# Group phases of a hybrid decoder step: another order of eight units, and two smaller edits

## Chip, cores and metric

One NeuronCore of one Trainium2 chip runs the whole kernel. The metric is device time in microseconds (us), the median of three runs.

## What is computed

One layer of a hybrid decoder for a prompt (256 tokens) and 8 sequences of 8 tokens (64 samples), 320 columns in all, in float32. The change touches the Mamba-2 (SSD) branch alone. Cut to that:

```python
xbc, _ = causal_conv(xbc, sconv0, s_conv_w, s_conv_b)      # 24 tiles of 128 channels, 4 taps
xbc = silu(xbc)
xs, Bm, Cm = xbc[..., :2048], xbc[..., 2048:2560], xbc[..., 2560:]     # 4 groups of 8 heads of 64
cum = cumsum(dt * A)                                        # per head
lmat = exp(where(mask, cum[:, None] - cum[None, :], -inf))
cb = einsum('btgn,bsgn->btsg', Cm, Bm)
y = einsum('btsg,btsge,bsgep->btgep', cb, lmat, xs * dt) + exp(cum) * (Cm @ h)
h_new = exp(cum[-1]) * h + einsum('bsgn,bsge,bsgep->bgepn', Bm, exp(cum[-1] - cum), xs * dt)
gated = (y + D * xs) * silu(z)                              # then a norm per group, and w_pb
merged = sigmoid(ga) * ya + sigmoid(gb) * yb                # then w_out
```

x, z, xbc, ga and gb all come from products with slices of one weight matrix `w_in`.

## The kernel before

Activations lie with channels on 128 partitions and the 320 columns along the free dimension. A *unit* is one 128-channel output tile of a product with weights: `dense` (24 matmuls of 128x320: high weights by high input, high by low, low by high, since each float32 factor is split in two rounded parts). The list of units, in the order in which they run, is written by hand in `unit_order`; every engine loops over the same list. PE's queue is in order: a unit's matmuls, then what was placed behind that unit. In the loops over units, ScalarE (ACT) makes the high half of the weights two units ahead once the current unit is done (`high_ahead`, line 1541), then empties the unit's PSUM bank; VectorE (DVE) makes the low half behind it (`low_ahead`, line 2113). Each panel of weights (two units) is brought by SyncE's queue (SP) into one of four ring slots once the slot's last unit has its low half.

Four *group phases*, one for each SSD group `gr`, run from 724 to 941 us, eight units each (`PHASE_UNITS`, `four_each`). Phase 0: four units of xbc, then ga 0 to 3; phases 1 and 2: four of xbc, then z 0 to 3 or 4 to 7; phase 3: gb 0 to 3, then z 8 to 11. The four xbc units are convolved for the next group. An xbc unit costs ACT two copies into a padded buffer (`conv`), POOL three small copies (`conv_side`, lines 669 to 678), DVE four operations of 128x344 (`conv`, lines 2281 to 2285), and ACT a Silu in two pieces (`conv_silu`, lines 1684 and 1685), issued four units later. A gate unit (ga, z) costs ACT one activation into one of two buffers `gate_tmp` (`gate`, line 1896) and DVE one product (`gated`, line 2553). gb units are kept unopened.

Behind the units of a phase PE has the group's own work, by position `i` of the unit:

- `i` = 0: `group_rows`: inputs turned, the products cb, B turned; DVE makes xd (line 2615), xd_s (2621), and masked cb (`masked_scores`, 2646 to 2649).
- `i` = 0 to 3: `decay_rows(i)` for two heads; ACT takes three exponentials a head (`head_weights`, 1944 to 1946); DVE multiplies them by cb (`weights`, 2658 and 2660).
- `i` = 1 to 4: `head_outputs(i - 1)`, which waits for `weights(i - 1)`; DVE reads it out in `outputs` (2666).
- `i` = 1, DVE: `old_part` of the group before, `sample_masks` (2630 to 2637); `i` = 2, PE: `grown_decays`.
- `i` = 4 to 7: `sample_states(i - 4)`, of which the first waits for `outputs(3)`, the others for `update` of the step before (DVE, eight operations, 2681); POOL sends each updated state (line 787); `i` = 5: `prompt_states`.

SP loads the states of the next group into the four buffers that POOL has sent, in front of the panels named in `states_before`.

In `head_outputs` the two heads of a pair write the two halves of the partitions. The prompt's parts have 128 rows; the samples' part has 64: `xd_s[0:64]` by `w[0:64, 384:448]`. Each float32 matmul shows as two in the profile.

Of the kernel before, what the change touches and what calls it, by code (L numbers as in the profile page):

```python
# [6 lines left out]
ACT = mybir.ActivationFunctionType  # L7
# [128 lines left out]

def unit_order():
# [13 lines left out]
    order += [u for phase in PHASE_UNITS for u in four_each(phase)] + four_each(TAIL_UNITS)  # L151
# [30 lines left out]
def build(nc, io, out):  # L182
# [5 lines left out]
    with ctx:  # L188
# [292 lines left out]
        def phase_units(gr):  # L481
            return [st.at[name, q] for name, q in four_each(PHASE_UNITS[gr])]
# [23 lines left out]
        def _(sp_):  # L506
# [49 lines left out]
            states_before = {("xbc", 2): (0, 1, 2, 3), ("z", 2): (4, 5), ("xbc", 12): (6,), ("xbc", 14): (7,), ("z", 6): (8, 9),  # L556
# [33 lines left out]
        def _(pool):  # L590
# [184 lines left out]

            picks(0, 0)
            for gr in range(SG):
                for i, u in enumerate(phase_units(gr)):
                    if u.name == "xbc":
                        conv_side(u, pad2, 3)  # L780
                    if i < 4 and (gr, i) != (SG - 1, 3):
                        picks(gr + (i + 1) // 4, (i + 1) % 4)
                for j in range(4):
                    n = 4 * gr + j
                    pool.wait_ge(S["up_done"], n + 1)
                    for s in range(2):
                        pool.dma_start(h_of(out["s_ssm"], j + 4 * s, gr), four(state_of(n, s))).then_inc(state_out[n % 4], 16)
                    if j == 1:
                        pool.wait_ge(S["ph_copied"], gr + 1)
                        pool.dma_start(h_of(out["p_ssm"], 0, gr), four(prompt_h)).then_inc(prompt_sent, 16)  # L790
# [29 lines left out]
        def _(pe):  # L820
# [506 lines left out]
            def head_outputs(gr, i):  # L1327
# [15 lines left out]
                for o, col, w in heads:  # L1343
                    ins = mm(b[o, 256:320], xd_s[0:64, col], w[0:64, 384:448], False, True)
# [178 lines left out]
        def _(act):  # L1523
# [373 lines left out]

            def kept_gate(u, func):
                act.wait_ge(unit_done, u.done)
                nc.scalar.activation(merged_g[:, u.own, :], bank_of(u), func).then_inc(bank_free[u.bank], 1)  # L1900
# [32 lines left out]
            def head_weights(gr, i):  # L1933
# [6 lines left out]
                for e in range(2):  # L1940
# [5 lines left out]
                    nc.scalar.activation(w[0:64, 384:448], aux[e][0:64, 384:448], ACT.Exp, bias=g3[0:64, 2, 4 + h:5 + h]).then_inc(S["w_exp"], 1)  # L1946
# [17 lines left out]
            for gr in range(SG):  # L1964
                us = phase_units(gr)
                for i, u in enumerate(us):
# [9 lines left out]
                    else:  # L1976
                        gate(u, ACT.Sigmoid if u.name == "ga" else ACT.Silu)
# [16 lines left out]
                    if i >= 4:  # L1994
                        if us[i - 4].name == "xbc":
                            conv_silu(us[i - 4], acc2, xbc_t)
# [93 lines left out]
        def _(dve):  # L2090
# [488 lines left out]
            def decay_halves():  # L2579

                ch.inc(V.tensor_copy(cum_rows[64:96, 0:256], aux[0][0:SH, 0:256]))
# [69 lines left out]
            def weights(gr, i):  # L2651

                dve.wait_ge(S["w_exp"], 8 * gr + 2 * i + 2)
                if i == 0:
# [3 lines left out]
                ch.inc(V.scalar_tensor_tensor(out=w[:, :, 0:384], in0=w[:, :, 0:384], scalar=1.0, in1=c[:, :, 0:384].to_broadcast([128, 2, 384]),  # L2658
                                              op0=ALU.min, op1=ALU.mult))
                V.scalar_tensor_tensor(out=w[0:64, :, 384:448], in0=w[0:64, :, 384:448], scalar=1.0, in1=c[0:64, :, 384:448].to_broadcast([64, 2, 64]),  # L2660
                                       op0=ALU.min, op1=ALU.mult).then_inc(S["w_ready"], 1)
# [35 lines left out]
            for gr in range(SG):  # L2697
                for i, u in enumerate(phase_units(gr)):
                    low_ahead(u)
                    if u.name == "xbc":  # L2700
                        conv(u, pad2, 3, acc2, 216, 240, 24)
# [11 lines left out]
                    if i == 4:  # L2713
                        weighted_inputs(gr)
                    if i >= 4:
                        update(gr, i - 4)
                        gated(u, ya if u.name == "ga" else xbc_t)
# [38 lines left out]
            dve.wait_ge(S["gate_open"], 1)  # L2756
# [75 lines left out]
```

## Time and profile before

| | us |
|---|---|
| median of 3 runs (lowest, highest) | 1340.95 (1337.51, 1342.23) |
| the profiled execution's own time | 1340.6 |
| its span | 1338.9 |
| TensorE (PE) busy | 1272.0, 95% |
| VectorE (DVE) busy | 768.1, 57% |
| ScalarE (ACT) busy | 617.7, 46% |
| GpSimd (POOL) busy | 215.4, 16% |

The span is the time between the first and the last instruction. The 1.7 us between span and time lie outside. A row of a timeline gives the start and length of a run of equal instructions, and in brackets how long the engine sat idle before it and whose result released it. `arena` is one large buffer that holds most of the branch's tiles, so its name says little; the line tells the operation.

### The profile page before, as it was taken

How to read it: one execution, taken by the hardware profiler on the slowest of the kernel's cores; microseconds unless marked ns; L12 is line 12 of the kernel's file. 1: busy time of each engine (PE TensorE's matmuls, PEld its weight loads, DVE VectorE, ACT ScalarE, POOL GpSimd, SP SyncE). 2: the span in 40 equal slices, each digit the busy share in tenths (PEclk: the TensorE clock that was granted, in tenths of full speed). 3: DMA queues.
4: the chain of work that ended last, by engine and by line, in shares of the span. 5: the costliest groups of instructions: out<-in, count | busy, mean ns of one | idle time of the engine just before them, and what ended most of it. 6: DMA issues, size and time to landing. Idle time of an engine off the chain costs nothing. (4 is left out here: it accounts for less than half of the span.)

```text
span 1338.9 us, 22662 instructions
## 1 busy us (share of the span) xinstructions
PE 1272.0 (95%) x9096; PEld 1157.1 (86%) x9096; DVE 768.1 (57%) x1340; ACT 617.7 (46%) x1066; POOL 215.4 (16%) x377
## 2 busy tenths in 40 slices
PE   6899999998999999989999999999999999999997
PEld 3799999997997776668998888888989979999997
DVE  1644445336885565655379786865665565545433
ACT  3433333334667554644355664554652343333443
POOL 3100000001540321211024242321500010000010
PEclk9899999998999999999999999999999989999999
DMA  9957677785443688893764355473436465544551
GB/s 301 265 182 230 221 221 212 224 235 179 127 127 127 199 273 291 290 282 106 203 196 128 119 173 167 134 213 114 126 94 189 142 205 158 154 137 131 152 149 42
DMA packets 258862, 241.56 MB, mean 180 GB/s; under 512 B 8607, under 2 KB 242479, under 8 KB 258710
## 3 DMA queue, kind: packets, MB, share of 16 engines
q1 hardware_dynamic: 249262, 211.03, 52.0%
q0 software_dynamic: 9024, 28.91, 6.3%
q8 instruction: 73, 1.20, 0.4%
q10 hardware_dynamic: 472, 0.17, 0.1%
q14 instruction: 31, 0.25, 0.1%
HBM read 209.88 MB, written 30.21 MB: 179 GB/s over the span
## 5 line engine op out<-in xcount | busy, mean ns | idle before, releaser
L2113 DVE TENSOR_TENSOR w_lo<-ring,w_hi 128x1024 fp32r<-128x1024 f32 (+1 forms) x264 | 336.8, 1277 | 421.1 <-ACT w_hi L1541 420.6
L1541 ACT ACTIVATE w_hi<-ring 128x1024 fp32r<-128x1024 f32 (+1 forms) x264 | 289.3, 1097 | 532.3 <-PE bank L826 526.2
L826 PE MATMUL bank<-u_hi,w_hi 128*128 128x320 f32 x1536 | 275.4, 323 | 9.6 <-ACT u_hi L1566 5.1
L826 PEld LDWEIGHTS bank<-u_hi,w_hi 128*128 128x128 f32 x1536 | 238.2, 193 | 28.3 <-issue 19.5
L826 PE MATMUL bank<-u_lo,w_hi 128*128 128x320 f32 x1536 | 257.6, 310 | 0.0
L826 PE MATMUL bank<-u_hi,w_lo 128*128 128x320 f32 x1536 | 257.0, 310 | 0.1
L826 PEld LDWEIGHTS bank<-u_lo,w_hi 128*128 128x128 f32 x1536 | 234.8, 189 | 0.0
L826 PEld LDWEIGHTS bank<-u_hi,w_lo 128*128 128x128 f32 x1536 | 233.7, 188 | 0.6 <-DVE w_lo L2113 0.4
L628 POOL TENSOR_TENSOR arena<-arena 128x320 f32<-128x320 f32 x24 | 21.0, 874 | 611.8 <-ACT arena L1553 598.8
L823 PE MATMUL aux<-ident,arena 128*128 128x128 f32 (+6 forms) x404 | 61.8, 278 | 17.3 <-ACT arena L1598 8.7
L826 PE MATMUL bank<-arena 32*128 32x128 f32 (+5 forms) x536 | 57.5, 376 | 15.1 <-DMA arena<-in_state_mlstm_C 7.9
L823 PEld LDWEIGHTS aux<-ident,arena 128*128 128x128 f32 (+6 forms) x404 | 44.8, 143 | 30.5 <-issue 16.0
L826 PE MATMUL bank<-ff_hi,w_hi 128*128 128x320 f32 x352 | 58.5, 314 | 0.0
L826 PE MATMUL bank<-ff_lo,w_hi 128*128 128x320 f32 x352 | 56.8, 309 | 0.0
L826 PE MATMUL bank<-ff_hi,w_lo 128*128 128x320 f32 x352 | 56.8, 309 | 0.0
L826 PEld LDWEIGHTS bank<-arena 32*128 32x128 f32 (+3 forms) x536 | 30.4, 155 | 30.5 <-issue 17.8
L826 PEld LDWEIGHTS bank<-ff_hi,w_hi 128*128 128x128 f32 x352 | 52.3, 188 | 2.5 <-issue 2.5
L826 PEld LDWEIGHTS bank<-ff_lo,w_hi 128*128 128x128 f32 x352 | 52.9, 188 | 0.0
L826 PEld LDWEIGHTS bank<-ff_hi,w_lo 128*128 128x128 f32 x352 | 52.9, 188 | 0.0
L2283 DVE SCALAR_TENSOR_TENSOR arena<-arena,par 128x344 f32<-128x344 f32 x80 | 46.6, 583 | 6.6 <-POOL arena L675 4.3
L1527 ACT ACTIVATE arena<-bank 128x256 f32<-128x256 f32 (+4 forms) x138 | 44.4, 352 | 12.8 <-PE bank L826 9.4
L826 PE MATMUL bank<-y_hi,w_hi 128*128 128x320 f32 x256 | 43.2, 310 | 2.3 <-ACT w_hi L1541 1.3
(363 smaller groups left out, 1513.0 us busy)
## 6 DMA issues: line engine op xcount, KB each, us to landing
ring<-in_w_in SPq DMA_DIRECT2D x52, 1024.0 KB, 5.4
ring<-in_ff_w SPq DMA_DIRECT2D x44, 1024.0 KB, 5.5
ring<-in_ada_w SPq DMA_DIRECT2D x36, 1024.0 KB, 7.4
ring<-in_ff_w SPq DMA_DIRECT2D x32, 704.0 KB, 4.9
arena<-in_state_mlstm_C SPq DMA_DIRECT2D x32, 512.0 KB, 5.6
out_s_C<-arena POOLq DMA_DIRECT2D x32, 512.0 KB, 5.7
ring<-in_w_pa SPq DMA_DIRECT2D x8, 1024.0 KB, 8.1
arena<-in_state_ssm SPq DMA_DIRECT2D x32, 256.0 KB, 4.3
```

The source lines that it names most:

```text
L628: ins = nc.gpsimd.tensor_tensor(sq[:, 0, :], sq[:, 0, :], sq[:, kc, :], ALU.add)
L823: return nc.tensor.transpose(dst, src, ident[0:rows, 0:rows])
L826: return nc.tensor.matmul(dst, lhs, rhs, start=first, stop=last)
L1527: return nc.scalar.activation(dst, src, ACT.Copy, scale=scale)
L1541: nc.scalar.activation(w_hi[v.split_no % 2][:, 0:v.kc, :], panel_part(v), ACT.Copy).then_inc(S["hi_done"], 1)
L2113: V.tensor_tensor(w_lo[r][:, 0:v.kc, :], panel_part(v), w_hi[r][:, 0:v.kc, :].bitcast(FP32), ALU.subtract)\
L2283: ch.link(V.scalar_tensor_tensor(out=a, in0=p[:, tap:tap + CONVW], scalar=par[:, c + w_col + tap * tiles:c + w_col + tap * tiles + 1], in1 ...
```

## The change

Three edits.

1. Order. In phases 0 to 2 the two first gate units come first, then the four xbc units, then the other two gate units. Phase 3 stays. The first two gates are copied out of PSUM unopened; ACT opens them in place (Sigmoid or Silu) at `i` = 4, and DVE applies them at `i` = 5. At `i` = 4 DVE convolves behind `outputs(3)` and `weighted_inputs`, at `i` = 5 in front of `update(1)`. The Silus of the convolved tiles come at `i` = 5, 6 and (two) 7. POOL sends the first state at `i` = 5 in front of that unit's share of the convolution. The state loads keep their places in SP's queue.
2. The weights of a pair of heads are multiplied in one operation of 128x896 in place of one of 128x768 and one of 64x128.
3. For that, the samples' part of `head_outputs` has 128 rows, the exponentials of the samples run over 128 rows, and the lower halves of `xd_s` and of the samples' part of cb are cleared once (`decay_halves`).

```diff
+def phase_order(phase):
+    own, other = phase[0], phase[1]
+    if own[0] != "xbc":
+        return four_each(phase)
+    rest = four_each((other,))
+    return rest[0:2] + four_each((own,)) + rest[2:4]
...
-            states_before = {..., ("z", 2): (4, 5), ("xbc", 12): (6,), ("xbc", 14): (7,), ...
+            states_before = {..., ("z", 2): (4, 5), ("z", 4): (6,), ("xbc", 12): (7,), ...
...
 POOL, in the phases
+                    if i == 5:
+                        send_state(gr, 0)
                     if u.name == "xbc":
                         conv_side(u, pad2, 3)
...
-                for j in range(4):
+                for j in range(1, 4):
+                    send_state(gr, j)
...
 PE, head_outputs
-                    ins = mm(b[o, 256:320], xd_s[0:64, col], w[0:64, 384:448], False, True)
+                    ins = mm(b[o, 256:320], xd_s[:, col], w[:, 384:448], False, True)
...
 ACT
-                    nc.scalar.activation(w[0:64, 384:448], aux[e][0:64, 384:448], ACT.Exp, bias=g3[0:64, 2, 4 + h:5 + h]).then_inc(S["w_exp"], 1)
+                    nc.scalar.activation(w[:, 384:448], aux[e][:, 384:448], ACT.Exp, bias=g3[:, 2, 4 + h:5 + h]).then_inc(S["w_exp"], 1)
...
-                        gate(u, ACT.Sigmoid if u.name == "ga" else ACT.Silu)
+                        gate(u, ACT.Copy if i < 4 else gate_func(u))
...
-                    if i >= 4:
-                        if us[i - 4].name == "xbc":
-                            conv_silu(us[i - 4], acc2, xbc_t)
+                    if i == 4 and gr < SG - 1:
+                        for v in us[0:2]:
+                            x = gate_tmp[:, gate_no[v.n] % 2, :]
+                            nc.scalar.activation(x, x, gate_func(v)).then_inc(S["gate_open"], 1)
+                    if gr < SG - 1 and i >= 5:
+                        for v in us[i - 3:i - 2] if i < 7 else us[4:6]:
+                            conv_silu(v, acc2, xbc_t)
...
 DVE, decay_halves
+                ch.inc(V.memset(xd_s[64:128, :], 0.0))
+                ch.inc(V.memset(cbm[64:128, 384:448], 0.0))
...
 DVE, weights
-                ch.inc(V.scalar_tensor_tensor(out=w[:, :, 0:384], in0=w[:, :, 0:384], scalar=1.0, in1=c[:, :, 0:384].to_broadcast([128, 2, 384]), ...))
-                V.scalar_tensor_tensor(out=w[0:64, :, 384:448], in0=w[0:64, :, 384:448], scalar=1.0, in1=c[0:64, :, 384:448].to_broadcast([64, 2, 64]), ...)
+                V.scalar_tensor_tensor(out=w, in0=w, scalar=1.0, in1=c.to_broadcast([128, 2, 448]), op0=ALU.min, op1=ALU.mult).then_inc(S["w_ready"], 1)
...
 DVE, in the phases
-                    if u.name == "xbc":
+                    if u.name == "xbc" and i != 4:
                         conv(u, pad2, 3, acc2, 216, 240, 24)
...
                     if i == 4:
                         weighted_inputs(gr)
+                        if u.name == "xbc":
+                            conv(u, pad2, 3, acc2, 216, 240, 24)
                     if i >= 4:
                         update(gr, i - 4)
+                    if i == 5 and gr < SG - 1:
+                        for n, v in enumerate(phase_units(gr)[0:2]):
+                            dve.wait_ge(S["gate_open"], 2 * gr + n + 1)
+                            gated(v, ya if v.name == "ga" else xbc_t)
+                    if i >= 4 and u.name != "xbc":
                         gated(u, ya if u.name == "ga" else xbc_t)
```

## Rows read from the trace of the kernel before

**Rows 1.** The page, part 1: busy time and share of the span by engine.

```profile
...
PE 1272.0 (95%) x9096; PEld 1157.1 (86%) x9096; DVE 768.1 (57%) x1340; ACT 617.7 (46%) x1066; POOL 215.4 (16%) x377
...
```

**Rows 2.** Stretches of the span: phase 1.

```profile
...
777.80:833.00 55.20, 52.14 (x451) 45.90 (x450) 40.67 (x86) 28.41 (x67) 18.45 (x30) 1.00 0.52 158
...
```

**Rows 3.** Waits of PE from 723 to 942 us: total, times, longest (us).

```profile
...
PE bank L826 <- DVE arena L2660: 5.5, 8, 1.1
...
PE aux L826 <- DVE w_lo_rest L2637: 0.7, 2, 0.3
```

**Rows 4.** PE timeline: start, length, engine, line, operation, tiles [idle before <-releaser].

```profile
...
723.89 1.09 PE L823 MATMUL aux<-ident,arena 128*128 128x128 f32 x8 [1.78 <-ACT arena L1685]
...
732.72 0.87 PE L826 MATMUL bank<-arena 128*64 128x256 f32 x8 [0.88 <-DVE arena L2660]
...
777.85 1.04 PE L823 MATMUL aux<-ident,arena 128*128 128x128 f32 x8
...
787.02 0.87 PE L826 MATMUL bank<-arena 128*64 128x256 f32 x8 [1.06 <-DVE arena L2660]
...
793.69 0.87 PE L826 MATMUL bank<-arena 128*64 128x256 f32 x8 [0.38 <-DVE arena L2660]
...
804.29 0.87 PE L826 MATMUL bank<-arena 128*64 128x256 f32 x8 [0.57 <-DVE arena L2660]
...
806.74 0.49 PE L826 MATMUL bank<-arena 32*128 32x128 f32 x4 [0.29 <-DVE arena L2666]
```

**Rows 5.** DVE timeline in phase 1, iterations 0 and 1.

```profile
...
780.35 0.47 DVE L2281 TENSOR_SCALAR arena<-arena,par 128x344 f32<-128x344 f32 x1
...
782.58 1.28 DVE L2615 TENSOR_TENSOR arena<-aux,sp 128x512 f32<-128x512 f32 x2
...
785.82 0.96 DVE L2658 SCALAR_TENSOR_TENSOR arena<-arena 128x768 f32<-128x768 f32 x1
786.69 0.28 DVE L2660 SCALAR_TENSOR_TENSOR arena<-arena 64x128 f32<-64x128 f32 x1
...
```

**Rows 6.** ACT timeline: end of phase 0 and iteration 0 of phase 1.

```profile
...
775.83 1.28 ACT L1684 ACT_TABLE_LOAD   x1
...
777.45 0.24 ACT L1685 ACTIVATE arena<-arena 128x64 f32<-128x64 f32 x1
...
784.03 0.31 ACT L1946 ACTIVATE arena<-aux,g 64x64 f32<-64x64 f32 x1
...
```

**Rows 7.** PE timeline, one head output and the unit behind it.

```profile
743.98 0.60 PE L826 MATMUL bank<-arena 128*64 128x256 f32 x6
744.51 0.33 PE L826 MATMUL bank<-arena,xd_s 64*64 64x64 f32 x4
744.77 0.41 PE L826 MATMUL bank<-u_hi,w_hi 128*128 128x320 f32 x1
```

**Rows 8.** Groups of DVE by line and shape, the whole span: a clearing.

```profile
...
L2559 DVE MEMSET sp<- 64x32 f32 x1 | 0.1, 85 | 0.1
...
```

**Rows 9.** DVE timeline in the first eight convolved units: low halves.

```profile
...
685.99 1.22 DVE L2113 TENSOR_TENSOR w_lo<-ring,w_hi 128x1024 fp32r<-128x1024 f32 x1
...
709.44 1.22 DVE L2113 TENSOR_TENSOR w_lo<-ring,w_hi 128x1024 fp32r<-128x1024 f32 x1
...
719.79 1.23 DVE L2113 TENSOR_TENSOR w_lo<-ring,w_hi 128x1024 fp32r<-128x1024 f32 x1
...
```

**Rows 10.** DVE timeline in phase 0: the updates of iterations 4 and 5.

```profile
...
752.77 2.15 DVE L2681 SCALAR_TENSOR_TENSOR arena<-arena,h_dec,bank 128x128 f32<-128x128 f32 x8 [0.21 <-PE bank L826]
...
760.97 2.16 DVE L2681 SCALAR_TENSOR_TENSOR arena<-arena,h_dec,bank 128x128 f32<-128x128 f32 x8 [0.51 <-PE bank L826]
...
```

**Rows 11.** POOL timeline in phase 0: sending the first states.

```profile
...
755.50 1.60 POOL L787 DMA_DIRECT2D out_s_ssm<-arena  x2 [8.55 <-DVE arena L2681]
...
```

**Rows 12.** PE timeline in phase 0: second and third sample states.

```profile
...
759.76 1.16 PE L826 MATMUL bank<-arena 32*128 32x128 f32 x16
...
766.16 1.16 PE L826 MATMUL bank<-arena 32*128 32x128 f32 x16
...
```

More of the change, by code:

```diff
@@ L150, in unit_order @@
     order += [("xbc", q) for q in XBC_FIRST]
-    order += [u for phase in PHASE_UNITS for u in four_each(phase)] + four_each(TAIL_UNITS)
+    order += [u for phase in PHASE_UNITS for u in phase_order(phase)] + four_each(TAIL_UNITS)
     order += [("pb", q) for q in PART_ORDER]
@@ L481, in phase_units @@
         def phase_units(gr):
-            return [st.at[name, q] for name, q in four_each(PHASE_UNITS[gr])]
+            return [st.at[name, q] for name, q in phase_order(PHASE_UNITS[gr])]
         def tail_units():
@@ L554, in state_loads @@
                     sp_.dma_start(four(state_of(n, s)), h_of(io["state_ssm"], j + 4 * s, gr)).then_inc(state_in[r], 16)
-            states_before = {("xbc", 2): (0, 1, 2, 3), ("z", 2): (4, 5), ("xbc", 12): (6,), ("xbc", 14): (7,), ("z", 6): (8, 9),
+            states_before = {("xbc", 2): (0, 1, 2, 3), ("z", 2): (4, 5), ("z", 4): (6,), ("xbc", 12): (7,), ("z", 6): (8, 9),
                              ("gb", 0): (10,), ("gb", 2): (11,), ("z", 10): (12, 13), ("z", 12): (14,), ("z", 14): (15,)}
@@ L774, in picks, with send_state @@
                 pool.wait_ge(S["masks_ready"], MH + n + 1)
+            def send_state(gr, j):
+                n = 4 * gr + j
+                pool.wait_ge(S["up_done"], n + 1)
+                for s in range(2):
+                    pool.dma_start(h_of(out["s_ssm"], j + 4 * s, gr), four(state_of(n, s))).then_inc(state_out[n % 4], 16)
             picks(0, 0)
@@ L782, in _ @@
                         picks(gr + (i + 1) // 4, (i + 1) % 4)
-                for j in range(4):
[L784 to L787, printed above, removed]
+                for j in range(1, 4):
+                    send_state(gr, j)
                     if j == 1:
@@ L1896, in gate, with gate_func @@
                 nc.scalar.activation(gate_tmp[:, i % 2, :], bank_of(u), func).then_inc(bank_free[u.bank], 1)
+            def gate_func(u):
+                return ACT.Sigmoid if u.name == "ga" else ACT.Silu
             def kept_gate(u, func):
@@ L2657, in weights @@
                 c = cbm.unsqueeze(1)
[L2658 to L2661, printed above, removed]
+                V.scalar_tensor_tensor(out=w, in0=w, scalar=1.0, in1=c.to_broadcast([128, 2, 448]), op0=ALU.min, op1=ALU.mult).then_inc(S["w_ready"], 1)
             def outputs(gr, i):
@@ L2755, in _ @@
                 group_norm_low(c)
-            dve.wait_ge(S["gate_open"], 1)
+            dve.wait_ge(S["gate_open"], 2 * SG - 1)
             def merge(u):
```

## The prediction, made before the changed kernel ran

> **What bounds the kernel now.** I read the page first. PE is busy 95% of the span and no other engine above 57% [rows 1], so the order of PE's own queue sets the end, and time is won only where PE waits or where its own work gets shorter. Then I took the stretches of the four group phases. The reader is to see 55.2 us for phase 1 with 52.1 us of PE in it at a granted clock of 1.00, with DVE the next busiest [rows 2]: some 3 us a phase are not PE's, and the clock has nothing to give back there. Then PE's waits in the phases, where two groups matter: 5.5 us in 8 waits for the weights' second operation (line 2660) and 0.7 us in 2 for line 2637, the rows of `grown_decays` [rows 3]. Then PE's timeline, to place them [rows 4]: phase 0 has one of 0.88 us at the first head output; phase 1 has 1.06 (head output 0), 0.38 (head output 1), 0.57 (head output 3) and 0.29 (first sample states), and phase 2 repeats phase 1 to a hundredth. Phase 0 has the 0.57 and the 0.29 too. The last reading is why `weights` is late: in phase 1's iteration 0 DVE convolves from 780.35 to 782.58 (2.23 us), and only then reads the group's rows, with the weights' first operation at 785.82 and the second ending at 786.97 [rows 5], while the exponentials had ended at 784.34 [rows 6]. The convolution stands in front of the work that PE waits for.
>
> **The order of the units, what it removes.** In iterations 0 and 1 of phases 0 to 2 DVE loses one convolution each, 2.23 us. A gate unit there costs DVE nothing, and ACT one copy in place of two.
> Phase 1, iteration 0: weights(0) would start at 785.82 - 2.23 = 783.6, but the exponentials end at 784.34, so it starts near 784.4 and ends near 785.5. PE was ready for head output 0 at 787.02 - 1.06 = 785.96 [rows 4 to 6]. The wait of 1.06 goes, with 0.5 us to spare; next in line are the exponentials, in time.
> Iteration 1: DVE again is 2.23 us earlier. weights(1), whose end let PE start at 793.69, comes near 791.4. PE, without its waits of 1.06, 0.35 (0.7 in 2, [rows 3]) and 0.38, gets there near 793.69 - 1.79 = 791.9; the rows of `grown_decays` stand a weights operation ahead of it, and PE asks for them 0.7 us ahead, so they are as much in time. Both waits go, again by about 0.5 us.
> Phase 0: the 0.88 goes in the same way. Sum: 0.88 + 2 x (1.06 + 0.38) + 0.7 = 4.46 us, say 4.5.
>
> **What of the waits stays.** Iteration 3 still holds a convolution: ACT's high half, DVE's low half, 2.23 us of convolution and the weights follow the end of unit 3 as before, so head output 3 still waits about 0.57 us in phases 0 to 2. Behind it the first sample states wait for outputs(3), and that stands behind the low half that begins when unit 4 is done. So what head output 3 gains by itself is lost 1 us later in the 0.29 [rows 4]. I count nothing for either.
>
> **Where the convolutions go.** Iteration 4: 2.23 us now lie in front of update(0). It ran from 752.77 to 754.92 in phase 0 [rows 10]; it will end near 757.1, and PE wants it at 759.76, behind unit 5 and the prompt's states [rows 12]. Cover 2.6 us. Iteration 5: conv in front of update(1), which was done at 763.1 after 0.51 us of waiting [rows 10] and will be at 764.9 to 765.4; PE wants it at 766.16 [rows 12]. Cover 0.8 to 1.3 us. If either cover went, the excess would be paid once in each of three phases. The two late products of the opened gates (0.5 us each) come behind update(1), ahead of a low half that can't start before ACT has seen the unit in front of 766.16 done: nothing.
> POOL: sending the first states takes 1.60 us from 755.50 [rows 11]; it will start near 757.1 and stands in front of unit 5's history copy (an estimated half microsecond, by the length of such short POOL work), which ends near 759.2. DVE wants it behind its low half, at 760.97 - 0.51 = 760.46 [rows 10]. Cover 1.2 us. SP: the loads stand at the same panels, and their buffers are sent at most 2 us later; they are used a phase later. Nothing.
> ACT: the opening of two gates at iteration 4 is one table load (1.28, [rows 6]) and two activations of half a microsecond, 2.3 us; a Sigmoid's table load, gate and tile's Silu stood there before, and DVE asks for the gates only a unit later. Nothing. At iteration 7 there are two tiles of Silu where there was one. In phase 0 the gate there is a Sigmoid, so a table load from 775.83 stands ahead of the Silu, whose last piece ends at 777.69; PE turns the rows at 777.85 without a wait [rows 4, 6]. The tile took 777.69 - 775.83 - 1.29 = 0.57 us, and one more behind it, overlapping by 0.1, brings the end to 778.15 to 778.2: PE waits about 0.35 us. In phases 1 and 2 gate and Silu share a table and the 1.28 us are not there, so 0.9 us of room is left. Cost 0.35 us, once.
> A rule of the Trainium skill speaks against this place (page "ScalarE: Activation LUTs", section "What ACT_TABLE_LOAD costs"): a switch costs 1.28 us and then a drain of 1.38 us. By that, iteration 7 with its two switches could not be over by 777.69 as it is. The trace has 1.28 us of load and the function right behind it, so I take the row; with the page's price PE's wait there would be 3.1 us and the whole gain about 2.1 us.
>
> **The one operation of weights.** 128x896 in one is about 0.07 us shorter than the two, by the distance from 785.82 to the end at 786.97 (1.15 us) against the first operation's rate (some 1.09). It ends in waits that are gone or re-anchored: nothing on the path. Bounds: 0 to 16 x 0.07 = 1.1 us; I take 0.
>
> **The 128 rows of head outputs.** PE runs the samples' part as 64*64 tiles between 128*64 tiles and 128*128 ones. In the row group of six, the last pair starts at 744.58 - 0.27 = 744.31, and pairs of 128 columns follow each other by 0.11, as in the run of eight of 1.04 us ((1.04 - 0.27) / 7 = 0.11). The next would start at 744.42; the 64*64 pair starts at 744.51 [rows 4, 7]. So 0.09 us goes with the change of tile shape. With 128 rows the shape is that of the pair before, and only the change to 128*128 behind it is left. That counts in front of a unit or a re-anchored wait, so for head outputs 0, 1 and 2 of each phase, not 3: 12 x 0.09 = 1.1 us. The trace of before has no 128*64 pass behind another one on 64 columns in this place, so bounds: gain up to 0.20 us each (the whole distance), 2.4 us; loss of 0.02 each (longer weight loads), 0.2 us. I take 1.1, the measured gap.
> The Trainium skill has this as a rule (page "TensorEngine Tiling (Array Packing)", section "Key Properties"): changing the tiling mode, not just the tile, drains TensorE. The trace agrees with a gap of 0.09 us at each change; by the rule alone the gain would have the same sign and no size.
>
> **The clearing.** Two new DVE operations of 512 and 64 columns in front of the first convolution. The nearest row clears 64x32 in 0.085 us [rows 8]; at about 1 ns a column that is 0.5 to 0.7 us in all. DVE there runs back to back: from 685.99 to 709.44 it needs 3.35 us a unit, against PE's 3.52, and it only just catches up: from 709.44 to 719.79 are 10.35 us where three periods are 10.05 [rows 9]. That is 0.3 us of slack before the last convolution, whose Silu PE waits for at 723.89. So 0.3 to 0.4 us comes through; I take 0.35. Bounds 0 and 0.7.
>
> **The sum.** -4.5 - 1.1 + 0.35 + 0.35 = -4.9 us. Made against the profiled execution's own 1340.6 us (span 1338.9 and 1.7 around it) that is 1335.7; the median of the three runs is 0.35 higher, so 1336.0. Behind the phases nothing is anchored to an outside clock: weights are loaded when slots come free, and the shift is carried to the end.
>
> **Rivals.**
> A. *The tile change gives nothing* (the gap belongs to the short 64-column pass and not to the shape). For: the gap is seen only ahead of 64 columns in this place. Against: all changes of shape have a gap like it. Sum -3.8: 1337.1.
> B. *The stalls move to head output 2 and 3.* With iterations 0 and 1 free of waits, PE reaches the units with convolutions sooner. From the end of unit 2, ACT's high half is about 1.2 us, DVE's low half and convolution 3.35 [rows 9], the weights 1.09: 5.7. PE needs 787.02 to 793.69 less its 0.73 of waits, 5.9, and two more decay products, 6.4. Were DVE 1.5 us later than that, 0.8 us would return in each of three phases: -2.5, 1338.4. Against: both are counted from the same unit's end, and their lengths repeat from phase to phase.
> C. *The gain is absorbed behind the phases*, in a wait for weights or states: about 1340. For: SP's queue holds loads behind states that POOL must have sent. Against: with 3 us of PE's waits a phase [rows 2], the weights were there each time.
> D. *Slower.* POOL now sends states in front of a history copy that DVE's convolution of unit 5 needs, and update(1) is behind that. Place: iteration 5 of phases 0 to 2. Free until the send is 1.2 us later than I have it, and PE feels it 0.9 us later still. From 2.1 us PE waits one for one, three times; to lose more than 4.9 us, each send has to be 3.7 us late, so to take 5.3 us for 1.6. For: POOL's operations vary with DVE at work. Against: the sends are 1.5 to 1.6 throughout. Price then 1342 and more.
>
> **Chances.** Forecast 0.60, A 0.14, B 0.12, C 0.08, D 0.06. I predict 1336.0. The forecast's own range is 1334.5 to 1337.5; with A, B and part of C, and the bounds of tile change and clearing, 1333.8 to 1339.8. 0.3% is 4.0 us and about what a measurement of this kernel can tell from no change: faster by more needs under 1336.9. Most of the forecast and a little of A lie there: 0.56; the same 0.38; slower 0.06.
>
> **What would show it.** Right: PE has no wait at head outputs 0 and 1 in phases 0 to 2; it keeps 0.5 to 0.6 at head output 3 and 0.2 to 0.4 at the first sample states; a new wait of some 0.35 us on line 1685 at phase 1's rows; the first one, 1.78 us, grows to 2.1; the samples' part starts 0.11 behind the pair before it; phases 1 and 2 take 53.1 us for 55.2. Wrong: waits on the weights at head output 2, waits of `sample_states` for an update, DVE waiting for POOL at unit 5, or phases shorter by less than 1.5 us.

## The result and the profile after

| | before | after |
|---|---|---|
| median (lowest, highest; runs), us | 1339.57 (1335.23, 1342.23; 8) | 1331.95 (1325.47, 1339.78; 8) |
| the profiled execution's own time | 1340.6 | 1333.15 |
| its span | 1338.9 | 1331.4 |
| mean granted clock of TensorE | 0.985 | 0.986 |

The ratio is 0.9947 (95% interval 0.9929 to 0.9966): 7.6 us faster, between 4.6 and 9.5. The forecast of 1336.0 us had the direction right; the time is 1.85 us below its range. The kernel before has a median of 1339.57 now that it has 8 runs, 1.4 us less than the 1340.95 of the three that I worked from.

The page of the changed kernel answers to [rows 1]: PE is 3.0 us less busy, the span is 7.5 us shorter.

```profile
...
PE 1269.0 (95%) x9096; PEld 1156.7 (87%) x9096; DVE 767.7 (58%) x1326; ACT 618.0 (46%) x1070; POOL 205.8 (15%) x377
...
```

The stretches of the changed kernel, as in [rows 2]: phases 0 to 3 and then the twelve units up to `w_pb` (the tail). Columns: stretch and length, then PE, PEld, DVE, ACT and POOL busy (instructions), granted clock, DMA share, GB/s. Each phase begins where the next pass of PE could start behind the last unit before it.

```profile
...
720.09:776.52 56.43, 52.85 (x449) 46.76 (x447) 41.18 (x83) 36.28 (x75) 14.91 (x29) 0.97 0.40 124
776.52:829.65 53.13, 51.52 (x451) 46.02 (x450) 40.43 (x82) 29.63 (x71) 15.02 (x30) 1.00 0.56 162
829.65:882.37 52.72, 51.29 (x451) 45.96 (x449) 40.43 (x82) 29.37 (x69) 15.01 (x30) 1.00 0.56 170
882.37:935.32 52.95, 51.44 (x453) 46.16 (x451) 32.34 (x66) 26.48 (x55) 8.69 (x16) 1.00 0.52 155
935.32:987.48 52.16, 48.91 (x338) 47.17 (x336) 31.81 (x49) 34.85 (x54) 18.10 (x22) 1.00 0.43 125
...
```

Before, the same stretches were 55.90, 55.16, 55.15, 53.41 and 53.18 us, at clocks of 1.00, 1.00, 1.00, 1.00 and 0.97. Phase 0 and the tail of the kernel before:

```profile
...
721.95:777.85 55.90, 51.96 (x449) 45.65 (x448) 41.18 (x87) 38.18 (x76) 15.70 (x29) 1.00 0.42 128
...
941.57:994.75 53.18, 50.43 (x339) 48.69 (x337) 32.98 (x51) 35.75 (x55) 18.11 (x22) 0.97 0.43 126
...
```

Phases 1 and 2 are 2.0 and 2.4 us shorter; phase 1 takes the 53.1 us forecast for both, phase 2 0.4 us less. Phase 0 is 0.5 us *longer*, at a clock of 0.97, though its wait of 0.88 us at the first head output is gone. And the tail, in which the change moves nothing, is 1.0 us shorter, with its clock at 1.00 now.

PE's waits from 715 to 940 us, with the columns of [rows 3]. Of the 5.5 us in 8 waits on `weights`, 2.0 us in 3 are left (line 2681 is the one operation now), and the 0.7 us on the rows of `grown_decays` are gone.

```profile
...
PE aux L837 <- ACT arena L1699: 2.3, 2, 2.1
PE bank L840 <- DVE arena L2686: 2.2, 4, 1.1
PE bank L840 <- DVE arena L2681: 2.0, 3, 0.7
...
```

PE's timeline, as in [rows 4, 7]: the rows of phase 0 and what follows them, head output 3 and the first sample states of phase 0, the rows of phase 1, and a head output of phase 3.

```profile
...
722.39 1.14 PE L837 MATMUL aux<-ident,arena 128*128 128x128 f32 x8 [2.14 <-ACT arena L1699]
723.33 1.06 PE L837 MATMUL bank<-ident,arena 128*64 128x128 f32 x4
724.18 1.89 PE L840 MATMUL bank<-arena 128*128 128x256 f32 x6
...
747.89 0.87 PE L840 MATMUL bank<-arena 128*64 128x256 f32 x8 [0.66 <-DVE arena L2681]
...
750.25 1.16 PE L840 MATMUL bank<-arena 32*128 32x128 f32 x16 [0.35 <-DVE arena L2686]
...
776.87 1.09 PE L837 MATMUL aux<-ident,arena 128*128 128x128 f32 x8 [0.18 <-ACT arena L1699]
...
890.41 0.87 PE L840 MATMUL bank<-arena 128*64 128x256 f32 x8
891.11 0.28 PE L840 MATMUL bank<-arena,xd_s 128*64 128x64 f32 x4
891.33 0.85 PE L840 MATMUL bank<-u_hi,w_hi 128*128 128x320 f32 x4
```

The same six products at phase 0's rows in the kernel before, behind its wait of 1.78 us:

```profile
...
725.26 1.08 PE L826 MATMUL bank<-arena 128*128 128x256 f32 x6
...
```

The reader is to see four things. The first wait is 2.14 us for the 1.78 of [rows 4], as forecast. No wait is left at head outputs 0 to 2; the two forecast to stay are there. The samples' part of head outputs (64 columns) has the shape of the pairs in front of it and starts 0.70 us after the first of them. And the six products at 724.18 take 1.89 us, for 1.08 before (725.26). That last row is what the forecast had no term for. The stretch from 723.3 to 726.7 of the changed kernel, with the columns of the stretches above, is at half clock (1.2 GHz for 2.4):

```profile
...
719.00:723.30 4.30, 2.16 (x17) 1.89 (x16) 2.64 (x5) 1.52 (x4) 2.15 (x5) 1.00 0.62 191
723.30:726.70 3.40, 3.40 (x16) 2.73 (x14) 3.38 (x5) 0.31 (x1) 0.00 (x0) 0.50 0.21 67
726.70:730.00 3.30, 2.87 (x18) 2.57 (x18) 0.89 (x4) 3.05 (x8) 0.58 (x2) 1.00 0.01 2
```

PE had sat idle for 2.14 us before it. In the kernel before, the wait there was 1.78 us and the clock stayed at full; its only fall between 720 and 1050 us is at 990.9, in the tail, behind waits of 1.01, 0.25 and 1.49 us.

Beside PE, in the changed kernel: DVE's weights(0) of phase 0 and its convolution at iteration 5, POOL's send and the history copy that rival D named, and ACT's Silus at the end of phase 0.

```profile
...
730.56 1.09 DVE L2681 SCALAR_TENSOR_TENSOR arena<-arena 128x896 f32<-128x896 f32 x1 [2.97 <-ACT arena L1963]
...
759.04 0.47 DVE L2302 TENSOR_SCALAR arena<-arena,par 128x344 f32<-128x344 f32 x1
...
756.08 1.60 POOL L789 DMA_DIRECT2D out_s_ssm<-arena  x2 [6.25 <-DVE arena L2701]
757.67 0.22 POOL L677 COPY arena<-hist 128x24 f32<-128x24 f32 x1
...
774.50 1.28 ACT L1698 ACT_TABLE_LOAD   x1
775.79 0.42 ACT L1698 ACTIVATE arena<-arena 128x256 f32<-128x256 f32 x1
...
776.57 0.24 ACT L1699 ACTIVATE arena<-arena 128x64 f32<-128x64 f32 x1
...
```

And the two clearings, by group (mean in ns):

```profile
...
L2602 DVE MEMSET xd_s<- 64x512 f32 x1 | 0.5, 485 | 0.2 <-issue 0.2
...
L2603 DVE MEMSET arena<- 64x64 f32 x1 | 0.1, 112 | 0.0
...
```

### The profile page after: what moved, and what is told of

Its sections match the earlier page's. It is cut to its first block, busy times and chain, and to the rows that moved or that the text cites. A ratio compares the mean times of both kernels' runs of the same rounds, so it can differ in the third digit from the quotient of the medians.

```text
span 1331.4 us, 22658 instructions
## 1 busy us (share of the span) xinstructions
PE 1269.0 (95%) x9096; PEld 1156.7 (87%) x9096; DVE 767.7 (58%) x1326; ACT 618.0 (46%) x1070; POOL 205.8 (15%) x377
## 4 chain that ended last, share of the span: by engine, by line
PE 55%; DVE 7%; ACT 4%; DMA 3%; issue 2%; POOL 0%; ACTq 0%; DVEq 0%; POOLq 0%
PE bank L840 47%; PE aux L840 6%; DVE w_lo L2134 2%; PE aux L837 2%; DMA arena<-in_state_mlstm_C 2%; ACT w_hi L1555 1%; DMA out_s_C<-arena 1%; DVE arena L2304 1%; DVE arena L2504 1%; PE bank L837 1%; ACT arena L1541 0%; ACT kp L1541 0%; DVE arena L2302 0%; DVE stats L2528 0%; ACT vp L1541 0%
```

## Experiments

Times are medians; the ratio is to the kernel before on the same chip. Since single executions scatter by 5 to 14 us, I read the terms from the profiles: "phases" is the sum of the four, "rest" the length from the start of phase 0 to the end of the last matmul (the kernel ends 6.5 to 6.9 us behind it in every profile). Before: phases 219.62, rest 610.26. After: 215.23 and 604.76.

| run | median (runs) | ratio, interval | phases 0, 1, 2, 3 | tail | rest |
|---|---|---|---|---|---|
| e1_after_again | 1332.39 (6) | 0.9955, 0.9941 to 0.9970 | 56.43 53.13 52.73 52.95 | 51.68 | 604.26 |
| e2_order_only | 1333.71 (6) | 0.9961, 0.9946 to 0.9976 | 54.95 53.58 53.18 53.39 | 53.69 | 606.28 |
| e3_rows_only | 1339.21 (12) | 0.9997, 0.9984 to 1.0011 | 57.14 54.75 54.75 52.94 | 52.31 | 610.13 |
| e4_clear_early | 1332.96 (6) | 0.9948, 0.9930 to 0.9965 | 54.51 53.12 52.74 52.95 | 53.70 | 604.39 |
| e5_fill_rows | 1333.93 (12) | 0.9963, 0.9946 to 0.9981 | 55.74 53.13 52.73 52.95 | 52.13 | 604.03 |
| e6_fill_all | 1330.68 (8) | 0.9941, 0.9919 to 0.9963 | 55.74 in phase 0 | 52.61 | 603.77 |
| e7_conv_late | 1329.67 (6) | 0.9935, 0.9915 to 0.9955 | 54.40 52.26 52.25 52.35 | 51.43 | 599.99 |
| e8_all | 1331.24 (7) | 0.9948, 0.9929 to 0.9968 | 54.74 52.27 52.27 52.36 | 52.61 | 600.85 |
| e9_late_early | 1330.83 (6) | 0.9913, 0.9882 to 0.9944 | 54.03 52.25 52.26 52.35 | 52.19 | 600.37 |
| e10_fill_sized | 1329.80 (6) | 0.9909, 0.9886 to 0.9933 | 54.04 52.25 52.26 52.35 | 51.57 | 599.06 |
| e11_two_weights | 1337.32 (1) | one run | 56.54 53.12 52.73 52.95 | 53.70 | 606.55 |

**e1_after_again**: the changed kernel, no edit, to learn how much of the result repeats.

> The changed kernel once more, for its spread and for the granted clock of each run. Theory (fixed gain in the phases plus TensorE's clock): between runs the time moves with the mean granted clock by about 1.6 us for 0.001, as the eight runs so far do (1325.5 us at 0.991, 1339.8 us at 0.982); the median is 6 to 8 us under before, and at equal clock the distance is 5 to 6 us. In the phases of its trace the only waits are again 0.65 us at head output 3, 0.35 at the first sample states (three times each), 0.2 at phase 1's rows and about 2.1 at phase 0's rows. Rival (all of the 7 us is fixed work saved): the distance at equal clock is 7 to 8 us.

Measured: 6.4 us under the kernel before (4.0 to 7.9). The phases repeat to a hundredth, the fall of the clock behind the first wait with them, and the tail again has no fall. The 17 executions of the kernel before on this chip and the 6 of this run have nearly the same mean clock (0.9866 and 0.9863) and mean times of 1338.6 and 1333.0 us. Within the runs of one kernel the time moves by some 1.4 us for 0.001 of mean clock, so my estimate of the distance at equal clock is 6.0 us, give or take 0.7: the upper end of the 5 to 6 expected.

**e2_order_only**: the changed kernel with the second and third edit taken back.

```diff
-                    ins = mm(b[o, 256:320], xd_s[:, col], w[:, 384:448], False, True)
+                    ins = mm(b[o, 256:320], xd_s[0:64, col], w[0:64, 384:448], False, True)
...
-                ch.inc(V.memset(xd_s[64:128, :], 0.0))
-                ch.inc(V.memset(cbm[64:128, 384:448], 0.0))
...
-                V.scalar_tensor_tensor(out=w, in0=w, ...)
+ (the two operations of before)
```

> Only the order of the units with what goes with it; the two weights operations, the 64-row samples' part and no clearing, as before. Theory: the waits at head outputs 0 and 1 and at grown_decays go (4.5 us), phase 1's rows wait 0.2 us, so 4.3 us under before at equal clock; phases 1 and 2 take 53.3 us where before has 55.2; the wait at phase 0's rows stays 1.78. Rival (the rows edit carries the part that was not forecast): the same 4.3, but then the rows alone give 3.

**e3_rows_only**: the opposite, the kernel before with the second and third edit alone.

> Only the one weights operation, the 128 rows and the clearing, in the old order. Theory: each head output is 0.14 us shorter on PE (0.10 ahead of the samples' part and 0.04 in it), of 16 some 10 to 12 count: 1.4 to 1.7 us, and the wait at phase 0's rows grows by 0.36; the weights end 0.07 us earlier, which shortens seven waits: 0 to 0.5 us. Sum 1.0 to 1.8 us under before at equal clock. Rival: 3 us.

Measured: the order is worth 219.62 - 215.10 = 4.5 us of phases, and 5.1 us of the medians (3.2 to 7.2). The other two edits are worth 0.04 us (219.62 - 219.58), and 0.9997 as a ratio: the 1.0 to 1.8 us expected of them did not come. The stretches show why: first e2_order_only's phases 0, 1 and 3, then e3_rows_only's.

```profile
...
720.17:775.12 54.95, 51.89 (x449) 45.56 (x447) 41.05 (x87) 36.13 (x75) 14.54 (x29) 1.00 0.42 129
775.12:828.70 53.58, 52.11 (x451) 45.94 (x450) 40.66 (x86) 29.48 (x71) 15.02 (x30) 1.00 0.53 160
...
881.88:935.27 53.39, 52.04 (x453) 46.08 (x451) 32.57 (x70) 26.35 (x55) 8.68 (x16) 1.00 0.53 156
...
```

```profile
...
720.38:777.52 57.14, 52.87 (x449) 46.68 (x448) 41.26 (x83) 38.30 (x76) 16.91 (x29) 0.97 0.41 126
777.52:832.27 54.75, 51.50 (x451) 45.95 (x450) 40.45 (x82) 28.53 (x67) 17.85 (x30) 1.00 0.52 159
...
887.02:939.96 52.94, 51.43 (x453) 46.16 (x451) 32.33 (x66) 26.49 (x55) 8.69 (x16) 1.00 0.52 154
...
```

In phase 3, where the order is the old one in both, 128 rows bring 53.41 to 52.94 and 53.39 to 52.95: 0.45 us for three head outputs, 0.15 each. So rival A is out. Phase 0 pays it back: 57.14 for 55.90, with the clock at 0.97, though no order was changed there. So the loss in phase 0 belongs to the third edit.

**e4_clear_early**: the changed kernel; `xd_s` is cleared behind unit 11 of `w_pa`, where DVE waits for about 2 us in each unit.

```diff
-                ch.inc(V.memset(xd_s[64:128, :], 0.0))
...
+                if u.q == 11:
+                    ch.inc(V.memset(xd_s[64:128, :], 0.0))
```

> The changed kernel with the large clearing (64x512) moved from in front of the first convolution to the units of w_pa before. Theory: the wait at phase 0's rows falls back from 2.14 to about 1.8 us; 0.3 us less at equal clock. If the clock falls after waits of PE and a longer wait makes it likelier, the half-clock stretch of 3.4 us that began at 723.3 us in the changed kernel is gone here in the profile and the mean clock of the runs is higher by 0.001 or so. If it is a matter of chance, the stretch may as well stay.

PE's timeline of e4_clear_early at the rows of phase 0:

```profile
...
718.66 1.09 PE L837 MATMUL aux<-ident,arena 128*128 128x128 f32 x8 [1.77 <-ACT arena L1699]
...
720.03 1.08 PE L840 MATMUL bank<-arena 128*128 128x256 f32 x6
...
```

Measured: the wait is back at 1.77, the six products at 1.08, phase 0 at 54.51 for 56.43. Of these 1.92 us, 0.36 is the wait (2.14 - 1.78) and 1.56 the clock. The time of the whole does not follow: the median of 1332.96 us is no lower than the 1332.39 of e1_after_again on the same chip, and the runs' mean clock is 0.9867 for 0.9863, where 0.001 more was expected. In this profile the tail has its fall of the clock again (53.70), as e2_order_only and e11_two_weights have, and before.

**e5_fill_rows**: the changed kernel with the wait left as it is, but with six float32 products in it whose results nothing reads, so that PE isn't idle. It separates "the wait got longer" from "PE idle lets the clock fall".

```diff
+            def fill(bank, n):
+                for k in range(n):
+                    mm(bank[:, 0:T], ones[:, :], x_t[:, 0, :], True, True)
...
                 if gr == 0:
                     pe.wait_ge(S["hd_read"], 1)
+                    fill(aux[2], 6)
+                pe.wait_ge(S["conv_silu"], 28 + 4 * gr)
```

> The changed kernel with six float32 products of 128x320 by ones (12 passes, 1.8 us of PE) put into the 2.1 us in which PE waits at phase 0's rows; their result is overwritten. Theory A (the clock falls because PE sat idle there): the half-clock stretch at 723 us is gone, the phase-0 stretch, 56.43 us from one unit's end to the next, falls to 54.8 to 55.0 although no wait of the data got shorter, and the stretch of half clock in the tail, which before, the order alone and the early clearing had at 980 to 991 us and the changed kernel had not, either comes back (then the two are tied, and nothing is won in all) or stays away (then 1.5 us are won). Theory B (the fall has nothing to do with the idle time): phase 0 stays at 56.4.

PE's timeline of e5_fill_rows:

```profile
...
722.30 3.39 PE L840 MATMUL aux<-x_t,ones 128*128 128x320 f32 x12
725.53 1.04 PE L837 MATMUL aux<-ident,arena 128*128 128x128 f32 x8
726.40 0.60 PE L837 MATMUL bank<-ident,arena 128*64 128x128 f32 x4
726.84 1.08 PE L840 MATMUL bank<-arena 128*128 128x256 f32 x6
...
```

Measured: no fall, with Silu as late as in the changed kernel. But twelve passes take 3.23 us to the next start where the gap was 2.30 (720.09 to 722.39), 0.9 us too long, so phase 0 gains 0.7 and not 1.6. The tail's fall stays away (52.13). So the 1.6 us come with the idle PE and not with the late data: the data are as late here. That rests on this profile and on e6_fill_all, which has the same fill and no fall there either.

**e6_fill_all**: the same fill, and further ones in front of the two norms' first units (8 products each) and of tail units 9 and 11 (4 each), where PE also waits.

> As e5_fill_rows, and the same kind of products in front of the two norms' first units (8 each, where PE waits 2.8 and 2.3 us for the normed input and the clock then falls for 6.8 and 3.4 to 6.8 us) and in front of the tail's units 9 and 11 (4 each, where it waits 1.5 us). Theory A: the half-clock stretches at 317, 723, 985 and 1085 us are gone or shorter, the mean clock goes from 0.987 to 0.993, and the time falls by 5 to 9 us under the changed kernel with no data wait changed. Theory B: the clock falls as before and the time is the same or, where a filler is longer than the wait, up to 1 us more.

Measured: mean clock 0.994 for 0.986 in the profiled executions; the `up2` units went from 158.14 to 156.13 us, but the fills in front of them were longer than the gap (41.12 us from the first unit of `w_out` to the first of `up2`, for 39.54). In all 1.0 us less rest than the changed kernel, and 3.3 us by the medians against e5_fill_rows on the same chip; 5 to 9 had been expected. Much of what the clock gave, the oversized fills took.

**e7_conv_late**: to take the two waits that stay. The convolution of iteration 3 goes behind `outputs(2)`, `outputs(3)` in front of the low half, and the Silus come as 1, 2, 1 at `i` = 5, 6, 7.

```diff
+                    if i == 4:
+                        outputs(gr, 3)
                     low_ahead(u)
-                    if u.name == "xbc" and i != 4:
+                    if u.name == "xbc" and i not in (3, 4):
...
-                    if 1 <= i <= 4:
+                    if 1 <= i <= 3:
                         outputs(gr, i - 1)
+                    if i == 3 and u.name == "xbc":
+                        conv(u, pad2, 3, acc2, 216, 240, 24)
...
-                        for v in us[i - 3:i - 2] if i < 7 else us[4:6]:
+                        for v in us[2:3] if i == 5 else us[3:5] if i == 6 else us[5:6]:
```

> The changed kernel with the two waits that I had let stand taken away: DVE convolves unit 3 behind outputs(2), reads head output 3 out in front of the next low half, and the Silus come one at i = 5, two at 6, one at 7. Theory (these waits are fixed work of DVE in front of what PE waits for): the 0.65 and the 0.35 go in phases 0 to 2, the 1.08 in phase 3, and the 0.18 at phase 1's rows: 4.2 us less; phases 1, 2 and 3 take 52.0, 51.7 and 51.9 for 53.13, 52.73 and 52.95. Rival (update or the convolution of unit 4 is late next): new waits for DVE at the second sample states and less than 2 us.

PE's timeline of e7_conv_late at head output 3 and the first sample states of phase 0:

```profile
...
745.24 0.87 PE L840 MATMUL bank<-arena 128*64 128x256 f32 x8
...
747.86 1.16 PE L840 MATMUL bank<-arena 32*128 32x128 f32 x16 [0.61 <-DVE arena L2686]
...
```

Measured: phases 211.26, 4.0 us under the changed kernel, of which 1.6 is that the clock did not fall behind a wait of 2.15 us in this execution. The other 2.4 us are the edit's own: the wait at head output 3 is gone, phase 1's rows are in time, but 0.61 us now stands at the sample states, since they need `outputs(3)` as soon as PE gets there. A stall moved by one step, and I had not counted it: 4.2 us had been expected, and phases 1, 2 and 3 at 52.0, 51.7 and 51.9 us came out at 52.26, 52.25 and 52.35.

**e8_all**: early clearing, late convolution and the fills (5, 8, 8, 4, 4 products).

> Early clearing, late convolution, spread Silus and the fillers (five in place of six at phase 0's rows) together. If the parts add: 0.35 for the clearing, 4.2 for the waits, 5 to 9 for the clock, 10 to 13 us under the changed kernel and some 18 under before. If the clock falls on its own, 4 to 5 under the changed kernel.

Measured: the parts do not add. The rest is 3.9 us under the changed kernel's (10 to 13 expected), the median 6.6 us under the kernel before (18 expected).

**e9_late_early**: the same without fills.

> The late convolution, the spread Silus and the early clearing together, no fillers. Theory: phase 0 takes 54.0 us (54.41 with the late convolution alone, less 0.35), the others as in e7_conv_late (52.25, 52.25, 52.35); the clock has no fall at phase 0's rows; from the end of the last unit ahead of the phases to the last matmul 599.6 us where the tail keeps full clock and 601.1 where it falls there. The median 1329 to 1331. Rival (the 1.9 us of the clearing in e4 were chance): phase 0 keeps 55.6.

Measured: phase 0 takes 54.03 us, the others what they take in e7_conv_late, and the median is 1330.83, all as expected. The rest is 600.37 for 599.6.

**e10_fill_sized**: with the fills cut to the gaps (3, 4, 4, 2, 2).

> e9 with fillers cut to the waits: a product of 128x320 takes 0.53 us (two passes of 0.27), so 3 at phase 0's rows (1.6 us in 1.9), 4 in front of each of the two norms' first units (2.1 us in 2.8 and 2.3) and 2 in front of each of the two tail units (1.1 us in 1.5). Theory (the idle time lets the clock fall, and the fillers of e6 and e8 gave back 1 us and more each by being longer than the waits): no stretch of half clock at 317, 985 and 1085 us, none of the four waits longer than without fillers, and 3 to 6 us under e9. Rival (a shorter filler leaves enough idle time for the clock to fall): as e9 within 1 us.

Measured: e9's phases are 210.89, 4.3 us under the changed kernel. The fills of e8 cost what they win behind the start of phase 0 (rest 600.85 against 600.37 without). Cut to size they gain there: PE's timeline in front of the first norm's first unit, first e9_late_early, then e10_fill_sized:

```profile
...
320.90 5.48 PE L840 MATMUL bank<-u_hi,w_hi 128*128 128x320 f32 x16 [2.80 <-ACT u_hi L1580]
...
```

```profile
...
317.68 2.32 PE L840 MATMUL aux<-x_t,ones 128*128 128x320 f32 x8
320.65 4.30 PE L840 MATMUL bank<-u_hi,w_hi 128*128 128x320 f32 x16 [0.65 <-ACT u_hi L1591]
...
```

The same 16 passes take 4.30 us for 5.48, and they start as long after the pass before the wait as without the fill. From phase 0 on e10 is 1.3 us shorter than e9; the medians (1329.80 and 1330.83) can't tell them apart, so the 3 to 6 us expected did not come. Ahead of phase 0 this profile has a half-clock stretch at 443.6 us, behind a wait of 1.83 us, that no other profile has. e10_fill_sized has the lowest ratio, with an interval that overlaps those of e7_conv_late and e9_late_early: 10.0 us under the kernel before on its chip, and 5.7 us under the changed kernel by the rest (599.06 for 604.76). Its ratio's interval (0.9886 to 0.9933) just meets that of the changed kernel (0.9929 to 0.9966); the two were not timed on the same chip.

**e11_two_weights**: the changed kernel with the weights' operation cut into 128x768 and 128x128.

```diff
-                V.scalar_tensor_tensor(out=w, in0=w, ...).then_inc(S["w_ready"], 1)
+                ch.inc(V.scalar_tensor_tensor(out=w[:, :, 0:384], in0=w[:, :, 0:384], ...))
+                V.scalar_tensor_tensor(out=w[:, :, 384:448], in0=w[:, :, 384:448], ...).then_inc(S["w_ready"], 1)
```

> The changed kernel with its one weights operation split again in 128x768 and 128x128. Theory (the one operation is off the path): head output 3 waits 0.07 us longer and the first sample states 0.07 less, phases 1 to 3 stay at 53.13, 52.73 and 52.95 us within 0.05. Rival: each of the 16 is paid, 0.07 to 0.3 us a phase more.

PE's timeline of e11_two_weights at head output 3 and the sample states of phase 0:

```profile
...
750.16 0.87 PE L840 MATMUL bank<-arena 128*64 128x256 f32 x8 [0.72 <-DVE arena L2682]
...
752.46 0.79 PE L840 MATMUL bank<-arena 32*128 32x128 f32 x9 [0.28 <-DVE arena L2687]
```

Measured: phases 1 to 3 equal the changed kernel's to a hundredth. Head output 3 waits 0.07 us longer and the sample states 0.07 us shorter (0.72 and 0.28, for 0.66 and 0.35): the one operation is worth nothing on the path. The run's 1337.32 us is one execution, with the tail's fall (53.70) and a half-clock stretch of 6.8 us for 3.4 at the second norm.

## Why the prediction was wrong

**The step that failed** is the last one of the sum, and what it was laid on: "Made against the profiled execution's own 1340.6 us ... that is 1335.7; the median of the three runs is 0.35 higher, so 1336.0", with "the shift is carried to the end" behind it. I gave the unknown costs a width; the base and all that lies outside the phases got none, and the clock got no term at all. The base was 1.4 us high: with 8 runs the kernel before is at 1339.57, and on the other chips at 1338.76, 1337.85 and 1339.80 (17, 20 and 11 runs). That is 1.4 of the miss of 4.05 us. The other 2.7 us are a measured difference of 7.6 us where I had 4.95. Between the two profiles (spans 7.5 us apart) it divides so:

| | forecast | measured | from |
|---|---|---|---|
| waits removed | -4.46 | -4.9 | e2's phases -4.5, less the Silu |
| 128 rows, 12 head outputs | -1.1 | -1.8 | e2 against after, phases 1 to 3: 0.45, 0.45, 0.44; e4 gives the same in phase 0 |
| Silu at phase 1's rows | +0.35 | +0.4 | phase 1 less phase 2, after |
| clearing, the wait | +0.35 | +0.36 | 2.14 - 1.78 |
| clearing, the clock behind it | not seen | +1.6 | e4: 1.92 - 0.36 |
| the four phases | -4.9 | -4.4 | 219.62 to 215.23 |
| behind them | 0 | -1.1 | 390.64 to 389.53 |
| ahead of them | 0 | -1.9 | 721.95 to 720.09 |

*The phases.* Their total is off by 0.5 us, by two errors that nearly cancel, gains 1.1 us too small and a loss of 1.6 us not seen; that it came so close is luck. The waits removed are worth 0.06 us more apiece than the brackets say: they measure idle time from the modelled end of the pass before. At phase 1's rows the bracket says 0.18 us (776.87), and the start is 0.35 us later than back to back (776.52, where the next pass could have started). So the forecast of 0.35, made from the end of the Silu, was right, and reading 0.18 would have made it seem wrong.

*The 128 rows.* The mechanism was right, the size off: I took the 0.09 us in front of the 64-column part (it starts 0.80 us after the first pass of the eight in the profile before, 0.70 now) and missed a second piece behind it, where the unit starts 0.22 us after that part for 0.26 (891.11 to 891.33, and 744.51 to 744.77 in [rows 7]). Together 0.14. The Trainium skill's page "TensorEngine Tiling (Array Packing)", section "Key Properties", has the drain at a change of tiling mode. At this place the runs agree, and put 0.14 to 0.15 us on one 64*64 part between 128*64 tiles and a 128*128 one. But I was wrong to write of a gap "at each change", and under rival A that "all changes of shape have a gap like it". In the kernel before, at phase 1's rows, eight 128*128 passes from 777.85, four 128*64 ones and then 128*128 again follow each other at the even distance of 0.11 us:

```profile
...
778.73 0.60 PE L823 MATMUL bank<-ident,arena 128*64 128x128 f32 x4
779.16 1.08 PE L826 MATMUL bank<-arena 128*128 128x256 f32 x6
...
```

There is no gap at either change (0.88 us for eight, 0.43 for four). Which changes have one stays open.

*The clearing.* The wait came out as forecast (485 + 112 ns of clearing, 0.36 us let through; the units of [rows 9] are twelve, not eight). What it let loose was not in my sum: the reader of [rows 2] finds me writing that "the clock has nothing to give back there", which looks at the clock as a gain only. A wait of 1.78 us of PE, made 2.14, put 3.4 us at half clock behind it. Over all profiles with PE idle there: four of the five with 2.13 to 2.15 us have the fall (after, e1, e3, e11; not e7), none of the four with 1.77 or 1.78 (before, e2, e4, e9). Filled, with the Silu just as late, it does not come (e5 and e6). e8 and e10 say nothing on this, since their clearing is early. Why e7 has no fall stays open.

*Behind and ahead of the phases.* "Nothing anchored behind" holds: the stretch from the first unit of `w_out` to the first of `up2` is 39.54 us in both. The -1.1 us is the clock again: the tail's fall at 990.9 is not in the changed profile (-1.0), and at the second norm it stands 3.4 us at half clock for 6.8 (-0.4), with +0.3 in the last units. I don't count this for the change: e2, e4 and e11, which hold the new order too, have the tail's fall. Nor the -1.9 us ahead, where no instruction was changed; over all profiles that part takes 715.9 to 723.3 us, and the changed kernel's variants lie at both ends. So this pair of profiles shows 4.4 us in the phases, while the timed differences are 7.6 and 6.4 us, with intervals (4.6 to 9.5, 4.0 to 7.9) of which the first just misses 4.4. The timed runs fit the terms without the clock better: -4.9 - 1.8 + 0.4 + 0.36 is -5.9, and the estimate at equal clock in e1_after_again is 6.0. The mean clock of all 14 executions of the changed kernel (0.9868) is no lower than that of the 48 of the kernel before on the three other chips (0.9864), where a further fall of 3.4 us in each would take off 0.0013 (the standard error of the 14 is 0.0006). So over many runs the fall at phase 0's rows is either not in each, or others are fewer, as the tail's is in the profiles of after and e1; which of the two stays open. By this reading, which is an estimate, the change itself is worth about 6 us, and the miss of 4.05 us is 1.4 of base, some 1.1 of gains sized too small and some 1.6 of scatter.

**What was right.** No wait at head outputs 0 to 2: weights(0) of phase 0 starts at 730.56 right behind the exponentials and ends at 731.65, 0.2 us before PE comes (731.83). The samples' part starts 0.11 us behind the pair before it. Head output 3 waits 0.65 (0.5 to 0.6 forecast, 0.57 in e2), the first sample states 0.35. Rival B is out: nothing waits at head output 2. Rival C is out, since the phases' gain is not met by a longer wait behind. Rival D is out: POOL sends at 756.08 in 1.60 us, the history copy ends at 757.89, and DVE asks for it at 759.04. The page "ScalarE: Activation LUTs" of the Trainium skill (section "What ACT_TABLE_LOAD costs") would have a drain of 1.38 us behind a table load; here the Silu starts 1.29 us after the load began (774.50 to 775.79), and phase 1's rows waited 0.35 us and not 3.1: the rows decide against that figure.

## What to carry to other kernels

Convolutions and other work without a near reader belong behind the operation that PE's queue asks for next; in this kernel that was worth 4.5 us and could be read off the timelines to half a microsecond. Before anything is put into PE's longest wait, even 0.4 us, ask what the clock does behind it: here the fall cost four times the wait itself in the profile, and with the wait the whole of what the third edit won, though the medians with and without it (e1, e4) can't be told apart. And a base of three runs needs a width of its own in the range, from the scatter of the runs: here 1.4 us, a third of the whole miss.

## Not expected of the hardware

- Half-clock stretches of 3.4 or 6.8 us stand at waits of PE of some 1.5 to 3.2 us, in a kernel with PE 95% busy: four to eight in every profile without fills, and part of one more at the very end. The one at phase 0's rows cost 1.56 us. Idle PE alone doesn't decide: a wait of 2.15 us had none behind it in e7_conv_late.
- Products that nobody reads, placed in such waits and not longer than them, kept the clock at 2.4 GHz there: 16 passes in 4.30 us for 5.48. For the whole kernel the medians show no gain from them (e9, e10). A float32 product of 128x320 is two passes of 0.27 us, 0.53 in all; six of them overran a gap of 2.3 us.
- The wait in brackets can be half of what the wait costs: 0.18 shown, 0.35 from start to start.
